# Moving the experts' weights in pieces of 4 MB instead of 2 MB

## The chip, the cores and the metric

The kernel runs on one core of one Trainium2 chip. The metric is the device time of one execution in microseconds (us). The kernel before takes 1259.34 us (median of 3 runs, 1258.63 to 1259.38).

## What is computed

One inference step of a one-layer hybrid encoder for 512 prompt tokens and 64 tokens of a running stream, model width 1024, all in float32:

```
proj = x @ w_in                                  # pool group, q, k, v, output gate, gate code
mix  = concat(pooling(u), gated_linear_attention(q, k, v, g)) @ w_out
h    = LN1(alpha * x + mix)
logits = h @ w_router + b_router                 # 32 experts, the top 4 of each token, softmax of the 4
for each expert e with its tokens:
    gate, up = split(h[tokens] @ w_gu[e] + b_gu[e])      # w_gu[e]: 1024 x 2048
    hmid = min(gate, 7) * sigmoid(1.702 * min(gate, 7)) * (clip(up, -7, 7) + 1)
    out  = hmid @ w_down[e] + b_down[e]                  # w_down[e]: 1024 x 1024
y    = LN2(alpha * h + sum over the 4 experts of weight * out)
```

Each expert has 8 MB of w_gu and 4 MB of w_down. All 32 experts are read, 384 MB.

## The kernel before, in words

The first part (projection, pooling, attention, w_out, LN1, router) takes the first 220 us. Then the experts follow in order, 0 to 31, with no branch between them; an expert has one block of at most 96 tokens (`BLK`), and further blocks, if any expert had more tokens, would be worked off in a loop behind them. Last, the rows of each token are fetched back from DRAM (`place`), summed and normalised in five groups.

**The ring.** The weights pass through SBUF in a ring of 8 slots (`RING`) of 2 MB, 16 KB per partition (`SLOT` = 4096 float32). An expert is 6 pieces (`PER`): pieces 0 to 3 are w_gu, 4 and 5 are w_down. Piece i of expert n lies in slot (6n + i) mod 8 (`piece_slot`). Each slot has a semaphore, `slot_in[s]`, that its transfer raises by 16; `landed(n, i)` is the count at which piece i of expert n is there. `EARLIER` counts the transfers of the first part (w_in) that used the same semaphores.

**Who issues.** SP issues all weight transfers, in order (`load`). Six go early, behind the last use of the ring's memory by the first part: pieces 0 to 3 of expert 0, and 0 and 1 of expert 1. Pieces 4 and 5 of expert 0 follow when the first rows of tokens are gathered. From then on each transfer waits for what lay in its slot 8 pieces before: a piece that is split is free when its two splits are done (`split_done`), piece 5, which the product reads as it is, when the down product of its expert is done (`down_read`).

**Who uses.** The multiplications run in float16 with a high and a low part. ACT makes the high part of 8 KB per partition at a time (a pair `p`, two to a piece, `hi`, L875), DVE the low part (`lo`, L1892), into 4 buffers each (`BUFS`). Of an expert pairs 0 to 7 are w_gu, 8 and 9 the first half of w_down. PE uses them in 16 units of 24 matmuls for gate and up (`unit`; units 2p and 2p+1 use pair p), and then the down product (`down`): 24 matmuls on pairs 8 and 9, and 16 float32 matmuls that read piece 5 from the ring. Before `down` of expert n PE transposes the gathered rows of expert n+1 (`rows`, L1347). DVE's order within an expert is written out in a loop at L1913: splits, with the small steps of gate and up (L1862, L1872, L1877) between them, and the low part of the next expert's rows (L1883).

**Beside it.** POOL gathers the rows of expert n+2 from DRAM (L678) and scatters the results of expert n (L691), with indirect transfers on a queue of their own (q0); the weights are on SP's (q1). Instructions are fetched over a third (q8). All share 16 DMA engines. When the down product of expert 30 is done, SP queues the loads of LN2's vectors and of `place`, behind the last weights.

Of the kernel before, what the change touches and what calls it, by code (L numbers as in the profile page):

```python
# [30 lines left out]
P = 128  # L31
D = 1024
KT = D // P
# [19 lines left out]
E = 32  # L53
# [4 lines left out]
SLOT = 4096  # L58
RING = 8
PER = 6  # L60
# [7 lines left out]
PAIRS = 10  # L68
# [6 lines left out]
def build(nc, x_prompt, x_sample, x_t, state_pool, state_gla, w_in, w_glr, w_pool, pool_scale, w_gate_up,  # L75
# [3 lines left out]
    with ExitStack() as ctx:  # L79
# [4 lines left out]
        ring = ctx.enter_context(nc.sbuf_tensor("ring", [P, RING * SLOT], F32))  # L84
# [194 lines left out]
        slot_in = [sem(f"slot_in{s}") for s in range(RING)]  # L279


        split_done, down_read = sem("split_done"), sem("down_read")
# [148 lines left out]
        def piece_slot(n, i):  # L431
            return (n * PER + i) % RING
# [6 lines left out]
        def landed(n, i):  # L439

            return 16 * (EARLIER[piece_slot(n, i)] + (n * PER + i) // RING + 1)

        def landed_again(b, i):

            return b * 16 + 16 * (EARLIER[i] + 1 + PER * E // RING)

# [24 lines left out]
        def _(sp):  # L471
# [43 lines left out]
            def load(e, i, s):  # L515

                src = w_gu[bass.ds(e, 1), i] if i < 4 else w_down[bass.ds(e, 1), i - 4]
                sp.dma_start(ring[:, s * SLOT:(s + 1) * SLOT], src.rearrange("a p n -> (a p) n"))\
                  .then_inc(slot_in[s], 16)
# [7 lines left out]
            sp.wait_ge(wo_lo, 8)  # L527
            for e, i in ((0, 0), (0, 1), (0, 2), (0, 3), (1, 0), (1, 1)):
                load(e, i, piece_slot(e, i))
# [5 lines left out]
            sp.wait_ge(gathered[0], 16)  # L535
            for i in (4, 5):
                load(0, i, piece_slot(0, i))
            for e in range(1, E):
                for i in range(2 if e == 1 else 0, PER):

                    if e == 2 and i == 0:
                        sp.dma_start(bd, b_down[0]).then_inc(bd_in, 16)

                    if i == 1:
                        sp.wait_ge(down_read, e - 1)
                    else:
                        sp.wait_ge(split_done, PAIRS * (e - 1) if i == 0 else PAIRS * (e - 1) + 2 * (i - 1))
                    load(e, i, piece_slot(e, i))
            sp.wait_ge(cnt_done, 1)
            more = sp.value_load(n_over_i[0:1, 0:1], min_val=0, max_val=E)  # L550
            with sp.If(more > 0):
                with sp.Fori(0, more) as b:
                    hold(sp, down_read, down_done(b + (E - 1)))
                    hold(sp, ov_known, b + 1)
                    e = sp.value_load(cur_i[0:1, 0:1], min_val=0, max_val=E - 1)
                    for i in range(PER):
                        load(e, i, i)
                hold(sp, down_read, down_done(more + (E - 1)))
                hold(sp, scattered, more * 16 + 16 * (E - 2))
# [173 lines left out]
        def _(act):  # L733
# [136 lines left out]
            def hi(n, p, s, got):  # L870

                if p % 2 == 0:
                    act.wait_ge(slot_in[s], got)
                act.wait_ge(unit_used, pair_done(n, p) - BUFS)
                act.activation(whi[buf(n, p)], packed(s, p), ACT.Copy, scale=W_UP).then_inc(hi_done, 1)  # L875
# [139 lines left out]
        def _(pe):  # L1015
# [359 lines left out]
            def down(n, s, got):  # L1375
# [17 lines left out]
                for k in range(first, KT):  # L1393
                    if k % 4 == 0:
                        pe.wait_ge(hm_done, n * 2 + (k // 4 + 3))
                        pe.wait_ge(slot_in[s[k // 4]], got[k // 4])
                    w = slot(s[k // 4], 4, 1024)
                    for c in range(2):
                        last = mm(out[:, c * 512:(c + 1) * 512], hm[:, k, :],
                                  w[:, k % 4, c * 512:(c + 1) * 512], k == 0, k == KT - 1)  # L1400
# [680 lines left out]
```

## Time and profile before

| | before |
|---|---|
| median of 3 runs | 1259.34 us |
| the profiled execution, its own time | 1259.37 us |
| its span on the profile | 1257.0 us |
| PE busy (weight loads) | 1192.7 us (867.1 us) |
| DVE busy | 1049.4 us |
| ACT busy | 944.6 us |
| moved by DMA | 475.17 MB, mean 378 GB/s |
| transfers of weights | 192 of 2048 KB |

Times in the rows below are from the start of the span. Busy shares are averages over parts of the kernel with different limits; what counts for this change is the stretch of the experts, from about 224 us to about 1210 us. PE's matmuls are pipelined and their ends modelled, so a busy PE isn't one at its peak. An idle time names what ended it. L1017 is the helper of all matmuls.

### The profile page before, as it was taken

To read this page: it belongs to the slowest core of one execution; us is meant where nothing else is said; L and a number is where in the kernel's file an instruction comes from. 1 tells how busy PE (TensorE), PEld (TensorE's weight loads), DVE (VectorE), ACT (ScalarE), POOL (GpSimd) and SP (SyncE) were. 2 spreads that over 40 slices of the span, in tenths; PEclk is the share of its full clock that TensorE was granted. 3 is DMA by queue.
4 is the path that set the end of the run, shared out by engine and by line. 5 is a ranking of instruction groups with operands and counts; after the bars stand their busy time and mean duration, and the time that the engine had idled before them with its cause. 6 is when DMAs were issued, how large, how long until landed. Compare 5 with 4: busy or idle time off the path is not lost.

```text
span 1257.0 us, 35029 instructions
## 1 busy us (share of the span) xinstructions
PE 1192.7 (95%) x15369; PEld 867.1 (69%) x15369; DVE 1049.4 (83%) x1209; ACT 944.6 (75%) x1260; POOL 172.2 (14%) x145
## 2 busy tenths in 40 slices
PE   7999998899999999999999999999999999999995
PEld 3555455777777777777777777777777777677752
DVE  6564577998899889898898898888888888888888
ACT  6532313688889888888888898888888888788841
POOL 1273111111000100000000011111111111111002
PEclk9999997899999999999999999999999999999998
DMA  9752491899999999999999999999999999999994
GB/s 367 291 197 86 144 406 36 355 406 421 426 425 424 424 427 424 424 425 426 425 425 425 424 426 424 424 425 426 424 426 424 425 424 425 422 422 426 409 395 139
DMA packets 47670, 475.17 MB, mean 378 GB/s; under 512 B 8781, under 2 KB 9812, under 8 KB 21660
## 3 DMA queue, kind: packets, MB, share of 16 engines
q1 hardware_dynamic: 35432, 438.69, 83.1%
q0 software_dynamic: 11392, 31.77, 6.7%
q8 instruction: 123, 2.02, 0.6%
q10 hardware_dynamic: 692, 2.43, 0.5%
q14 instruction: 31, 0.25, 0.1%
HBM read 453.17 MB, written 29.95 MB: 384 GB/s over the span
## 4 chain that ended last, share of the span: by engine, by line
PE 49%; DMA 28%; DVE 12%; issue 5%; ACT 5%; POOL 0%; DVEq 0%; SPq 0%; POOLq 0%; ACTq 0%
PE wide L1017 34%; DMA ring<-in_w_gu 16%; PE pair L1017 14%; DMA ring<-in_w_down 11%; DVE work L1892 6%; ACT work L875 3%; PE pair L1347 1%; ACT work L905 1%; DVE ring L1994 1%; DVE ring L2019 1%; DVE ring L2017 1%; DVE work L1877 0%; DMA ring<-in_x_t 0%; DVE ring L2006 0%; DMA work<-h_rows,work 0%
## 5 line engine op out<-in xcount | busy, mean ns | idle before, releaser
L1892 DVE SCALAR_TENSOR_TENSOR work<-ring,work 128x2048 f16<-128x2048 f32 x320 | 721.4, 2287 | 109.4 <-ACT work L875 94.5
L875 ACT ACTIVATE work<-ring 128x2048 f16<-128x2048 f32 x320 | 599.6, 1902 | 90.5 <-DMA ring<-in_w_gu 55.6
L1017 PE MATMUL wide<-work 128*128 128x96 f16 (+2 forms) x6970 | 465.2, 227 | 28.5 <-issue 12.6
L1017 PEld LDWEIGHTS wide<-work 128*128 128x128 f16 (+2 forms) x6970 | 364.7, 101 | 112.6 <-issue 42.2
L1017 PE MATMUL wide<-ring,work 128*96 128x512 f32 (+4 forms) x1024 | 335.1, 492 | 1.4 <-DMA ring<-part_rows 1.4
L1017 PEld LDWEIGHTS pair<-work 128*128 128x128 f16 (+2 forms) x6483 | 297.0, 100 | 34.6 <-issue 23.7
L1017 PE MATMUL pair<-work 128*128 128x96 f16 (+3 forms) x6483 | 303.5, 208 | 8.2 <-DVEq L1727 1.9
L1017 PEld LDWEIGHTS wide<-ring,work 128*96 128x96 f32 (+4 forms) x1024 | 132.0, 135 | 178.3 <-issue 125.6
L678 POOL DMA_INDIRECT work<-h_rows,work x32 | 58.4, 1826 | 477.7 <-PE pair L1347 450.4
L691 POOL DMA_INDIRECT part_rows<-work x30 | 43.1, 1438 | 373.2 <-ACT work L935 373.2
L905 ACT ACTIVATE work<-pair,work 128x96 f32<-128x96 f32 x256 | 64.8, 333 | 0.0
L905 ACT ACTIVATE work<-wide,work 128x96 f32<-128x96 f32 x256 | 64.8, 332 | 0.0
L935 ACT ACTIVATE work<-wide,work 96x1024 f32<-96x1024 f32 x30 | 33.1, 1103 | 38.6 <-PE wide L1017 38.4
L914 ACT ACTIVATE work<-work 128x384 f32<-128x384 f32 x64 | 39.4, 616 | 2.1
L921 ACT ACTIVATE work<-work 128x384 f32<-128x384 f32 x64 | 39.4, 616 | 2.1
L1872 DVE SCALAR_TENSOR_TENSOR work<-work 128x384 f32<-128x384 f32 x64 | 35.6, 556 | 1.3 <-DVE work L1862 0.2
L1347 PE MATMUL pair<-work 128*128 128x128 f32 x256 | 35.2, 282 | 0.6 <-DMA work<-h_rows,work 0.6
L1862 DVE SCALAR_TENSOR_TENSOR work<-work 128x384 f32<-128x384 f32 x64 | 35.3, 552 | 0.0
L1883 DVE SCALAR_TENSOR_TENSOR work<-pair,work 128x384 f16<-128x384 f32 x64 | 32.6, 549 | 1.1 <-ACT work L899 1.1
L1489 DVE SCALAR_TENSOR_TENSOR ring<-ring 128x1024 f16<-128x1024 f32 x16 | 19.3, 1224 | 14.2 <-ACT ring L771 13.9
L867 ACT ACTIVATE work<-pair 128x512 f32<-128x512 f32 (+1 forms) x10 | 5.0, 553 | 34.2 <-PE pair L1250 34.0
L899 ACT ACTIVATE work<-pair 128x384 f16<-128x384 f32 x64 | 27.3, 476 | 3.9 <-PE pair L1347 3.9
(211 smaller groups left out, 599.1 us busy)
## 6 DMA issues: line engine op xcount, KB each, us to landing
ring<-in_w_gu SPq DMA_DIRECT2D x128, 2048.0 KB, 29.9
ring<-in_w_down SPq DMA_DIRECT2D x64, 2048.0 KB, 30.7
part_rows<-work POOLq DMA_DIRECT2D x1, 10240.0 KB, 37.2
ring<-part_rows SPq DMA_DIRECT2D x5, 2048.0 KB, 31.4
ring<-in_w_in SPq DMA_DIRECT2D x3, 2048.0 KB
ring<-in_w_out SPq DMA_DIRECT2D x2, 2048.0 KB, 10.8
h_rows<-work POOLq DMA_DIRECT2D x1, 2560.0 KB, 9.9
ring<-h_rows SPq DMA_DIRECT2D x5, 512.0 KB, 20.0
```

The lines of the kernel that those rows point to most:

```text
L678: pool.indirect_dma_start(xg, None, h_dram, bass.IndirectOffsetOnAxis(ap=tok_i[q], axis=0), bounds_check=PLACES - 1, oob_is_err=False)\
L691: pool.indirect_dma_start(part_dram, bass.IndirectOffsetOnAxis(ap=dst_i[p], axis=0), orow, None, bounds_check=TOPK * PLACES - 1, oob_is_er ...
L875: act.activation(whi[buf(n, p)], packed(s, p), ACT.Copy, scale=W_UP).then_inc(hi_done, 1)
L905: last = act.activation(dst[:, c, :], b[:, c * BLK:(c + 1) * BLK], ACT.Relu, scale=-DOWN * S_UP, bias=bguT[:, at[0], at[1] + c:at[1] + c + 1])
L914: act.activation(sg, g1, ACT.Sigmoid, scale=-SWISH / S_UP, bias=sig_bias).then_inc(sig_done, 1)
L921: act.activation(u1, u1, ACT.Relu, scale=-1.0, bias=up_bias).then_inc(up_clip, 1)
L935: act.activation(orow, wide[1 if isinstance(n, int) else 0][0:BLK, :], ACT.Copy, scale=slots[p][:, 5:6])\
L1017: return pe.matmul(out, w, x, start=start, stop=stop, skip_group_check=True)
L1347: last = pe.transpose(bank[b][:, k * BLK:k * BLK + P], xg[:, (4 * b + k) * P:(4 * b + k + 1) * P], used)
L1862: dve.scalar_tensor_tensor(g1, g1, -LIMIT * S_UP, sg, ALU.add, ALU.mult).then_inc(gated, 1)
L1872: dve.scalar_tensor_tensor(hm[:, 4 * half:4 * half + 4, :], u1, (1.0 - LIMIT) * S_UP, g1, ALU.add, ALU.mult)\
L1892: dve.scalar_tensor_tensor(wlo[buf(n, p)], packed(s, p), W_UP, whi[buf(n, p)], ALU.mult, ALU.subtract).then_inc(split_done, 1)
```

## The change

The same bytes move in pieces of 4 MB, 32 KB per partition, each into a pair of neighbouring slots: (0,1), (2,3), (4,5), (6,7). An expert is three transfers instead of six: w_gu in two, w_down in one. In DRAM the two halves of a new piece are laid side by side for each partition (the layout is made on the host). `load` is called for even i only and writes two slots; the semaphore is that of the pair's first slot, and it is raised when all of the 4 MB are there. ACT's wait, before the high part of pairs 0, 2, 4, ..., is on that semaphore, and PE's wait for piece 5 on that of pieces 4 and 5. SP's waits are those of the later of the two slots: for the pair that held pieces 4 and 5 of an expert the end of its down product, else the second split of its second piece. The splits, their buffers and all matmuls stay as they are.

```diff
--- before.py
+++ after.py
@@ -438,11 +438,11 @@
 
         def landed(n, i):
 
-            return 16 * (EARLIER[piece_slot(n, i)] + (n * PER + i) // RING + 1)
+            return 16 * (EARLIER[piece_slot(n, i) // 2 * 2] + (n * PER + i) // RING + 1)
 
         def landed_again(b, i):
 
-            return b * 16 + 16 * (EARLIER[i] + 1 + PER * E // RING)
+            return b * 16 + 16 * (EARLIER[i // 2 * 2] + 1 + PER * E // RING)
 
         def pairs(n):
 
@@ -514,8 +514,8 @@
 
             def load(e, i, s):
 
-                src = w_gu[bass.ds(e, 1), i] if i < 4 else w_down[bass.ds(e, 1), i - 4]
-                sp.dma_start(ring[:, s * SLOT:(s + 1) * SLOT], src.rearrange("a p n -> (a p) n"))\
+                src = w_gu[bass.ds(e, 1), i // 2] if i < 4 else w_down[bass.ds(e, 1)]
+                sp.dma_start(ring[:, s * SLOT:(s + 2) * SLOT], src.rearrange("a p n -> (a p) n"))\
                   .then_inc(slot_in[s], 16)
 
             sp.wait_ge(o_norm, TILES)
@@ -525,7 +525,7 @@
             sp.wait_ge(z_out, 8)
             sp.wait_ge(states_out, 96)
             sp.wait_ge(wo_lo, 8)
-            for e, i in ((0, 0), (0, 1), (0, 2), (0, 3), (1, 0), (1, 1)):
+            for e, i in ((0, 0), (0, 2), (1, 0)):
                 load(e, i, piece_slot(e, i))
             sp.wait_ge(hT_ready, 2 * TILES)
             sp.wait_ge(h_stored, 16 * TILES)
@@ -533,18 +533,17 @@
 
             sp.wait_ge(mix_ready, TILES)
             sp.wait_ge(gathered[0], 16)
-            for i in (4, 5):
-                load(0, i, piece_slot(0, i))
+            load(0, 4, piece_slot(0, 4))
             for e in range(1, E):
-                for i in range(2 if e == 1 else 0, PER):
+                for i in range(2 if e == 1 else 0, PER, 2):
 
                     if e == 2 and i == 0:
                         sp.dma_start(bd, b_down[0]).then_inc(bd_in, 16)
 
-                    if i == 1:
+                    if i == 0:
                         sp.wait_ge(down_read, e - 1)
                     else:
-                        sp.wait_ge(split_done, PAIRS * (e - 1) if i == 0 else PAIRS * (e - 1) + 2 * (i - 1))
+                        sp.wait_ge(split_done, PAIRS * (e - 1) + 2 * i)
                     load(e, i, piece_slot(e, i))
             sp.wait_ge(cnt_done, 1)
             more = sp.value_load(n_over_i[0:1, 0:1], min_val=0, max_val=E)
@@ -553,7 +552,7 @@
                     hold(sp, down_read, down_done(b + (E - 1)))
                     hold(sp, ov_known, b + 1)
                     e = sp.value_load(cur_i[0:1, 0:1], min_val=0, max_val=E - 1)
-                    for i in range(PER):
+                    for i in range(0, PER, 2):
                         load(e, i, i)
                 hold(sp, down_read, down_done(more + (E - 1)))
                 hold(sp, scattered, more * 16 + 16 * (E - 2))
@@ -870,7 +869,7 @@
             def hi(n, p, s, got):
 
                 if p % 2 == 0:
-                    act.wait_ge(slot_in[s], got)
+                    act.wait_ge(slot_in[s // 2 * 2], got)
                 act.wait_ge(unit_used, pair_done(n, p) - BUFS)
                 act.activation(whi[buf(n, p)], packed(s, p), ACT.Copy, scale=W_UP).then_inc(hi_done, 1)
 
@@ -1393,7 +1392,7 @@
                 for k in range(first, KT):
                     if k % 4 == 0:
                         pe.wait_ge(hm_done, n * 2 + (k // 4 + 3))
-                        pe.wait_ge(slot_in[s[k // 4]], got[k // 4])
+                        pe.wait_ge(slot_in[s[0]], got[0])
                     w = slot(s[k // 4], 4, 1024)
                     for c in range(2):
                         last = mm(out[:, c * 512:(c + 1) * 512], hm[:, k, :],
@@ -2060,10 +2059,10 @@
     laid["w_out"] = np.asarray(inputs["w_out"])[0].reshape(2, 4, P, D).transpose(0, 2, 1, 3)
 
     laid["w_gu"] = np.asarray(inputs["w_gu"]).reshape(E, KT, P, 2, 2, 4, P).transpose(0, 4, 3, 2, 5, 1, 6)\
-        .reshape(E, 4, P, SLOT)
-
-    laid["w_down"] = np.asarray(inputs["w_down"]).reshape(E, 2, 4, P, D).transpose(0, 1, 3, 2, 4)\
-        .reshape(E, 2, P, SLOT)
+        .reshape(E, 2, 2, P, SLOT).transpose(0, 1, 3, 2, 4).reshape(E, 2, P, 2 * SLOT)
+
+    laid["w_down"] = np.asarray(inputs["w_down"]).reshape(E, KT, P, D).transpose(0, 2, 1, 3)\
+        .reshape(E, P, 2 * SLOT)
 
     laid["b_gu"] = np.asarray(inputs["b_gu"]).reshape(E, 16, P).transpose(2, 0, 1)
```

## Rows read from the trace of the kernel before

**Rows 1.** The page: slices of the span, and the queue of the weights (packets, MB, share).

```profile
DMA  9752491899999999999999999999999999999994
GB/s 367 291 197 86 144 406 36 355 406 421 426 425 424 424 427 424 424 425 426 425 425 425 424 426 424 424 425 426 424 426 424 425 424 425 422 422 426 409 395 139
q1 hardware_dynamic: 35432, 438.69, 83.1%
```

**Rows 2.** A window: length, PE, PEld, DVE, ACT, POOL busy, PEclk, DMA share, GB/s.

```profile
900.00:1000.00 100.00, 96.21 (x1400) 73.56 (x1399) 86.96 (x92) 84.97 (x105) 11.86 (x6) 1.00 1.01 425
```

**Rows 3.** The chain that ended last, experts 5 and 6: start, us, what.

```profile
402.25 12.25 PE wide L1017 x40
...
432.77 12.25 PE wide L1017 x40
```

**Rows 4.** ACT's timeline, experts 27 and 31: start, us, what, idle before and releaser.

```profile
1052.73 1.91 ACT L875 ACTIVATE work<-ring 128x2048 f16<-128x2048 f32 x1 [2.31 <-DMA ring<-in_w_gu]
...
1178.89 1.91 ACT L875 ACTIVATE work<-ring 128x2048 f16<-128x2048 f32 x1 [2.52 <-DMA ring<-in_w_gu]
...
1183.79 3.71 ACT L875 ACTIVATE work<-ring 128x2048 f16<-128x2048 f32 x2 [0.42 <-DMA ring<-in_w_gu]
```

**Rows 5.** Timelines of SP and ACT, the first loads.

```profile
0.81 0.43 SPq L474 DMA_DIRECT2D ring<-in_w_in  x1
...
4.93 1.06 ACT L771 ACTIVATE ring<-ring 128x1024 f16<-128x1024 f32 x1 [2.84 <-DMA ring<-in_w_in]
...
8.03 1.16 ACT L776 ACTIVATE work<-ring 128x1152 f16<-128x1152 f32 x1 [0.28 <-DMA ring<-in_x_t]
9.46 1.16 ACT L776 ACTIVATE work<-ring 128x1152 f16<-128x1152 f32 x1 [0.27 <-DMA ring<-in_x_t]
```

**Rows 6.** Expert 0: an issue and its landing, PE's and SP's timeline, the chain.

```profile
L518 SPq DMA_DIRECT2D ring<-in_w_down x1: 328/328/328, 240.2 to 240.2; - x1
...
DMA to landing us min/median/max: 13.3/13.3/13.3
...
247.17 1.07 PE L1347 MATMUL pair<-work 128*128 128x128 f32 x8
...
248.78 12.25 PE wide L1017 x40
...
250.90 10.96 SPq L518 DMA_DIRECT2D ring<-in_w_gu  x3
```

**Rows 7.** Gathers: the first (alone), the second, and those of 300 to 1180 us.

```profile
DMA to landing us min/median/max: 4.7/4.7/4.7
...
227.04 1.04 POOL L678 DMA_INDIRECT work<-h_rows,work  x1 [5.34 <-PE pair L1347]
...
DMA to landing us min/median/max: 10.5/11.9/12.9
```

**Rows 8.** The chain, expert 27: w_down taken up, and the down product.

```profile
1075.48 1.92 ACT work L875
...
1080.28 13.93 PE wide L1017 x40
```

**Rows 9.** The timeline of the last expert: DVE's steps, and PE's down product.

```profile
1183.05 1.01 DVE L1883 SCALAR_TENSOR_TENSOR work<-pair,work 128x384 f16<-128x384 f32 x2
...
1184.48 8.88 DVE L1892 SCALAR_TENSOR_TENSOR work<-ring,work 128x2048 f16<-128x2048 f32 x4
...
1193.29 1.27 DVE L1919 SCALAR_TENSOR_TENSOR work<-wide,work 96x1024 f16<-96x1024 f32 x1
...
1204.23 0.55 DVE L1877 SCALAR_TENSOR_TENSOR work<-work 128x384 f16<-128x384 f32 x1
...
1204.88 5.38 PE L1017 MATMUL wide<-work 128*96 128x512 f16 x24 [0.97 <-DVE work L1877]
```

**Rows 10.** DMA queues of 225 to 1180 us: packets, MB, share of 16 engines.

```profile
q0 software_dynamic: 7824, 18.04, 4.9%
q8 instruction: 107, 1.75, 0.7%
```

## The prediction, made before the changed kernel was run

> **What bounds the kernel now.** I read the page's slices first: from the tenth to the 37th the DMA digit is 9 and the rate stays at 421 to 427 GB/s [rows 1]. A window of 100 us sharpens it: the 16 DMA engines are busy the whole time, at 425 GB/s, beside a PE at 96, a DVE at 87 and an ACT at 85 [rows 2]. So from 224 us, when the second batch of weights starts, until the last weights land, the time is set by bytes. The compute is only slightly faster. In a stretch where the data are early, one expert takes 30.52 us (402.25 to 432.77 in the chain) [rows 3]. In a stretch where ACT waits for each piece, the first piece of an expert is taken up at 1052.73 (expert 27) and at 1178.89 (expert 31): 126.16 / 4 = 31.54 us per expert [rows 4]. The reader is to see two things: anything that leaves the DMA engines idle between 224 us and the last landing is paid in full, and the compute has 1.0 us of spare time in each expert, so a late start on the last expert isn't made up.
>
> **The rate (the term that gains).** The change sends the same bytes in half the transfers and half the rows. A 2 MB piece gives each of 16 engines 8 rows of 16 KB; with no gather on the queue two landings are 4.90 us apart (ACT starts at 1178.89 and 1183.79) [rows 4]. The x_t loads give each engine 8 rows of 4,608 bytes: landings 1.43 us apart (8.03, 9.46) [rows 5]. Two sizes with equal rows give the fixed part: bytes per engine 131,072 and 36,864; slope (4.90 - 1.43) / 94,208 = 0.0368 us per 1,000 bytes; fixed 1.43 - 36.9 x 0.0368 = 0.07 us (0.08 if either spacing is 0.01 off). Doubling the row saves that once per pair of old pieces. Of 96 new transfers 93 lie behind 224 us: 93 x 0.07 = 6.5 us. Bounds: 0, if a 32 KB row is cut in two again, and 7.5 us at 0.08. No row here is longer than 16 KB, so this is the largest unknown; I take 6.5, because each piece shows as exactly 128 large packets, one per row (35,432 packets for 438.69 MB) [rows 1].
> The Trainium skill (DMA: Bandwidth & Descriptors, Anatomy of one DMA) gives about 2 us fixed plus bytes at 436 GB/s for a transfer. The spacing above, 4.9 us where that rule has 6.8, shows that queued transfers here overlap all but 0.07 of it; by the rule the saving would be 96 x 2 = 192 us.
>
> **Issue times, start of the ring.** In the new order the wait for a pair of slots is that of its later half. (1,2) goes at the fourth split instead of the second, (1,4) at the eighth instead of the sixth: 5 us later each, behind work that still fills the queue. The exception is the pair whose old content is the down weights. Before, (2,0) is issued at 250.90, after the tenth split; (2,1) is the second of the three issues that follow, at the end of the down product, 248.78 + 12.25 = 261.03 [rows 6]. Now both go at 261.03. What is ahead: (1,4), issued 240.2, lands 13.3 us later [rows 6], at 253.5, and (1,5) 4.9 to 5.8 us on, 258.4 to 259.3; a gather shares the queue, so I say 259.5. A transfer into an empty queue has a start-up: the first w_in block is issued at 0.81 and taken up at 4.93 [rows 5], 4.1 us, of which its 512 KB take 1.2: 2.9. So the stream resumes at 261.03 + 2.9 = 263.9: idle for about 4 us (2.5 to 5.5 by the uncertainty of both ends). It is paid, as the DMA bounds the rest. The same pair of the next expert is released some 31 us later, at 292, and could be moving at 295; the stream, already 4 us late, is busy until 259.5 + 4 + 31.5 = 295: no second gap worth a term, and each further expert widens the cover by 31.5 - 30.5 = 1.0 us.
>
> **Gathers.** Alone a gather lands in 4.7 us; among weights in 11.9 (10.5 to 12.9) [rows 7]: about 7 us of waiting behind 16 KB rows. With rows of 32 KB I expect 7 more, 19. Each is issued right behind the transposes of one expert and wanted at those of the next, about 30 us on: hidden. Only the second, issued 227.0, has less: wanted at 247.17 [rows 6, 7], while 227 + 19 = 246. Cost nothing; were the cover gone, it would lengthen the gap above one for one, which the 5.5 holds. The Trainium skill (same page, Queues, rings and completion order) says that an engine changes between queues only at packet borders; the two gather times agree, and by it the doubling would be as reckoned.
>
> **The tail (the term that loses).** Both halves of a pair now raise one semaphore, so the first half is known one piece, 4.9 us, later. While the stream flows nothing is lost, as slots are refilled in time: at expert 27 w_down's first half is taken up at 1075.48, the down product ends at 1080.28 + 13.93 = 1094.21 [rows 8], 18.7 us later and about 13.8 behind the second half. Now that is some 19 behind the pair's landing, with three transfers (31.5 us) queued behind it: margin 31.5 - 19 - 2.9 = 9.6 us. At the end it is lost. For expert 31, DVE can begin when pieces 0 and 1 are there, 1183.79, and ACT has done 1.91: 1185.70. Up to the last f16 operand of the down product it has 9 splits at the pace of four in 8.88 (20.0), two f16 halves of the rows (1.0), places (the 0.4 between 1184.06 and 1184.48), the 1.27 of the previous expert's result, and three steps of 0.55 that overlap their neighbours a little (1.5): 24.2 us in a row [rows 9]. End 1209.9 against 1204.8 now, where the last of these steps (1204.23, 0.55) lets PE start at 1204.88 [rows 9]: 5.1, and with short waits between I take +5.5. PE is no help: its down product of expert 30 shifts by about as much. Bounds: 4.9 (one piece, if DVE has the rest to spare) and 7.5 (if the backlog of expert 30 adds to it). What follows the down product (PE's last sums, DVE's adding and normalising) starts from it; its loads are queued right behind the weights and land no later than now by more than the stream does, so the shift passes through.
> SP issues half as many transfers and queues nothing else in that time but b_down: nothing. ACT and PE run the same instructions, with some waits on another semaphore: nothing, hidden under DMA or DVE. The host's layout isn't in the time.
>
> **Sum.** The profiled execution took 1259.37 (span 1257.0 and 2.4 around it), against a median of 1259.34: no correction. 1259.4 + 4.0 - 6.5 + 5.5 = 1262.4. Ends of all terms: 1259.4 + 2.5 - 7.5 + 4.9 = 1259.3, and 1259.4 + 5.5 - 0 + 7.5 = 1272.4.
>
> **Rivals.**
> A. Long rows save nothing (cut to 16 KB): 1259.4 + 4.0 + 5.5 = 1268.9. For it: no longer row is seen; against: one packet per row so far. 0.18.
> B, other side: the fixed cost is larger than the quiet spacing tells. An expert takes 31.54, six quiet pieces 29.4, so 2.1 us go elsewhere; the gathers' and scatters' 18.04 MB over the 30.3 experts of that window are 0.60 MB or 1.4 us, instruction fetches (1.75 MB) 0.15 us [rows 10]. The 0.55 us left may be interruptions that go with the number of rows or transfers. If half vanishes: 31 x 0.28 = 9 us, 1253.4. It decides from 0.18 us per expert (1262.4 - 31 x 0.18 = 1256.8). For it: I can't place the 0.55; against: it may as well grow with long rows. 0.20.
> C. Four pairs starve the stream: the margin of 9.6 us is used up in some experts (the split chain, held until a whole pair is there, lags). At 0.5 us per expert 15 us more: 1278. Against: the margin. 0.11.
> D. The fixed cost is paid once per transfer, 2.9 us as in the start-up row: 1259.4 - 96 x 2.9 = 981. The rule of the Trainium skill cited above reads so; the quiet spacing contradicts it. 0.01.
>
> **From this to the numbers.** My own case has 0.50, 1259 to 1266. A change under 0.2% (2.5 us: 1256.8 to 1261.9) is about what can't be told from none. Of the 0.50 some 0.20 falls into that band. Faster: 0.20 + 0.01 = 0.21. Same: 0.20. Slower: 0.30 + 0.18 + 0.11 = 0.59. The range leaves out C and the lower half of B: 1253 to 1271; my case with A alone would be 1259 to 1271.
>
> **What would show it.** Rate: packets of 32 KB, quiet landings of pairs 9.7 us apart instead of 9.8. Start: a dip of the DMA share between 259 and 264. Ring: DMA share 1.0 from 270 to 1170. Gathers: landing near 19 us. Tail: the last w_down within 3 us of 1203.4 (now 1183.79 + 4 x 4.9), the last down product starting about 7 us behind it (now 1.5). I am wrong if a second gap shows (C), if packets stay at 16 KB (A), or if an expert takes under 31.1 us (B).

## The result, and the profile after

The changed kernel takes 1263.86 us (median of 5 runs, 1263.16 to 1265.51) against 1258.63 (5 runs, 1256.65 to 1259.38): a ratio of 1.0043, 95% interval 1.003 to 1.0056. Run again beside later experiments it was 1263.00 against 1258.95, 1.0030 (1.0019 to 1.0041). So it is 4 to 5 us slower, more than the 0.2% that counts as a difference here. The forecast was 1262.4, in a range of 1253 to 1271, with "slower" as the likeliest sign.

The profiled execution of the changed kernel took 1265.51, with a span of 1263.7. That is the longest of the five, so its trace holds a little more than the median does; what the second trace doesn't repeat is marked below.

From the page of the changed kernel: the slices, the weights' queue, the chain's shares by engine, and the issues of the weights. Behind SP's loads line numbers are one lower than before (L1016 is what was L1017).

```profile
DMA  9752491989999999999999999999999999999993
GB/s 357 301 193 86 166 383 34 359 365 417 389 417 430 424 419 428 432 429 427 424 429 426 417 427 429 428 428 426 429 426 427 426 423 427 425 428 428 419 390 105
...
q1 hardware_dynamic: 21608, 438.68, 82.3%
...
PE 84%; DVE 6%; DMA 5%; issue 3%; ACT 1%; POOL 0%; SPq 0%; DVEq 0%; POOLq 0%
...
ring<-in_w_gu SPq DMA_DIRECT2D x64, 4096.0 KB, 23.4
ring<-in_w_down SPq DMA_DIRECT2D x32, 4096.0 KB, 25.6
```

Three readings beside [rows 1]. The packets fell by 13,824. Of these 12,288 are the rows: 96 transfers of 128 instead of 192. The other 1,536 are 96 x 16, the small packets (under 512 B) that close a transfer on each of 16 engines. So a row of 32 KB is one packet. The rate of most slices of the flat part rose from between 424 and 426 GB/s to between 426 and 429, though single slices now fall to 417. Slices 9 and 11 fell to 365 and 389, where before they had 406 and 426. These slices, 253 to 284 us and 316 to 348 us, hold the start of the ring. And the chain changed its owner: before it was PE 49%, DMA 28%, DVE 12%, now PE 84%, DMA 5%.

**The start.** SP's timeline of the changed kernel, then windows of the same stretch (length, PE, PEld, DVE, ACT, POOL busy, PEclk, DMA share, GB/s).

```profile
245.12 0.33 SPq L518 DMA_DIRECT2D ring<-in_w_down  x1
...
261.46 2.07 SPq L518 DMA_DIRECT2D ring<-in_w_gu  x2
```

```profile
258.00:260.00 2.00, 2.00 (x6) 0.67 (x5) 2.00 (x2) 1.01 (x1) 0.00 (x0) 1.00 0.34 103
260.00:262.00 2.00, 2.00 (x22) 1.14 (x21) 2.00 (x2) 0.53 (x1) 0.00 (x0) 1.00 0.05 16
262.00:264.00 2.00, 2.00 (x52) 2.00 (x50) 1.98 (x6) 1.01 (x2) 0.51 (x1) 1.00 0.94 262
...
324.00:326.00 2.00, 2.00 (x6) 0.74 (x5) 2.00 (x2) 0.00 (x0) 0.00 (x0) 1.00 0.77 326
326.00:328.00 2.00, 2.00 (x29) 1.33 (x28) 2.00 (x3) 0.87 (x1) 0.00 (x0) 1.00 0.08 31
```

The issue that came at 250.90 [rows 6] comes at 261.46, and the queue is empty by then: the shares leave 2 x (0.66 + 0.95 + 0.06) = 3.3 us of idle DMA between 258 and 264 (before, the three shares were 1.02, 0.97 and 1.05). A second hole follows two experts later, 2 x (0.23 + 0.92) = 2.3 us at 326.

**The tail.** ACT's timeline, then DVE's, then the chain of the last expert of the changed kernel.

```profile
1185.73 1.91 ACT L874 ACTIVATE work<-ring 128x2048 f16<-128x2048 f32 x1 [2.56 <-DMA ring<-in_w_gu]
...
1195.44 1.91 ACT L874 ACTIVATE work<-ring 128x2048 f16<-128x2048 f32 x1 [0.65 <-DMA ring<-in_w_gu]
```

```profile
1191.32 8.88 DVE L1891 SCALAR_TENSOR_TENSOR work<-ring,work 128x2048 f16<-128x2048 f32 x4
...
1211.06 0.55 DVE L1876 SCALAR_TENSOR_TENSOR work<-work 128x384 f16<-128x384 f32 x1
```

```profile
1209.56 1.50 issue
1211.06 0.56 DVE work L1876
1211.62 0.09 issue
1211.71 12.25 PE wide L1016 x40
```

The pair is taken up at 1185.73; before, its second half was there at 1183.79 [rows 4], so the stream itself is 1.94 us late. The step of 0.55 us that frees the down product stood at 1204.23 and is now at 1211.06 [rows 9]; the product starts at 1211.71 instead of 1204.88, 6.83 later. Of these, 1.94 come from the stream and 4.89 from the tail. The last weights tell the same: they landed at 1203.4 before and at 1205.2 now (the last increment of their semaphore), and the product starts 6.5 behind that instead of 1.5. The spans differ by 1263.7 - 1257.0 = 6.7, so nothing is lost or won behind it. Take-up to down product: 26.0 us now (1185.73 to 1211.71), 21.1 before.

### The profile page after: what moved, and what is told of

Its sections match the earlier page's. It is cut to its first block, busy times and chain, and to the rows that moved or that the text cites. A ratio compares the mean times of both kernels' runs of the same rounds, so it can differ in the third digit from the quotient of the medians.

```text
span 1263.7 us, 34933 instructions
## 1 busy us (share of the span) xinstructions
PE 1191.1 (94%) x15369; PEld 869.3 (69%) x15369; DVE 1049.6 (83%) x1209; ACT 944.8 (75%) x1260; POOL 155.3 (12%) x145
## 4 chain that ended last, share of the span: by engine, by line
PE 84%; DVE 6%; DMA 5%; issue 3%; ACT 1%; POOL 0%; SPq 0%; DVEq 0%; POOLq 0%
PE wide L1016 58%; PE pair L1016 23%; DMA ring<-in_w_gu 4%; PE pair L1346 2%; DVE work L1891 1%; DVE ring L1993 1%; DVE ring L2018 1%; DVE ring L2016 1%; DMA ring<-in_x_t 0%; DVE ring L2005 0%; DMA work<-h_rows,work 0%; ACT work L874 0%; POOL work L664 0%; DVE work L1756 0%; DVE work L1766 0%
## 5 line engine op out<-in xcount | busy, mean ns | idle before, releaser
L874 ACT ACTIVATE work<-ring 128x2048 f16<-128x2048 f32 x320 | 598.2, 1902 | 71.4 <-DMA ring<-in_w_gu 37.4
L1016 PE MATMUL wide<-work 128*128 128x96 f16 (+2 forms) x6970 | 464.3, 227 | 31.9 <-issue 28.9
L1016 PEld LDWEIGHTS wide<-work 128*128 128x128 f16 (+2 forms) x6970 | 366.2, 101 | 112.4 <-issue 42.5
L1016 PE MATMUL wide<-ring,work 128*96 128x512 f32 (+4 forms) x1024 | 334.9, 492 | 0.0
L1016 PEld LDWEIGHTS pair<-work 128*128 128x128 f16 (+2 forms) x6483 | 297.5, 101 | 36.7 <-issue 26.2
L1016 PE MATMUL pair<-work 128*128 128x96 f16 (+3 forms) x6483 | 304.6, 208 | 9.7 <-issue 1.9
L1016 PEld LDWEIGHTS wide<-ring,work 128*96 128x96 f32 (+4 forms) x1024 | 132.2, 135 | 176.3 <-issue 125.6
L677 POOL DMA_INDIRECT work<-h_rows,work x32 | 43.5, 1361 | 515.2 <-PE pair L1346 485.6
L1346 PEld LDWEIGHTS pair<-work 128*128 128x128 f32 x256 | 28.2, 144 | 4.5 <-issue 4.5
L1488 DVE SCALAR_TENSOR_TENSOR ring<-ring 128x1024 f16<-128x1024 f32 x16 | 19.3, 1222 | 14.3 <-ACT ring L770 14.0
```

The source lines that it names most:

```text
L677: pool.indirect_dma_start(xg, None, h_dram, bass.IndirectOffsetOnAxis(ap=tok_i[q], axis=0), bounds_check=PLACES - 1, oob_is_err=False)\
L1016: return pe.matmul(out, w, x, start=start, stop=stop, skip_group_check=True)
L1346: last = pe.transpose(bank[b][:, k * BLK:k * BLK + P], xg[:, (4 * b + k) * P:(4 * b + k + 1) * P], used)
```

## The experiments

### The two new delays, each alone

In e2_order the kernel before keeps its 2 MB transfers and its semaphores; only SP's waits are those of the change.

```diff
-                for i in range(2 if e == 1 else 0, PER):
+                for i in range(2 if e == 1 else 0, PER, 2):
...
-                    if i == 1:
+                    if i == 0:
                         sp.wait_ge(down_read, e - 1)
                     else:
-                        sp.wait_ge(split_done, PAIRS * (e - 1) if i == 0 else PAIRS * (e - 1) + 2 * (i - 1))
+                        sp.wait_ge(split_done, PAIRS * (e - 1) + 2 * i)
                     load(e, i, piece_slot(e, i))
+                    load(e, i + 1, piece_slot(e, i + 1))
```

> The kernel before, 2 MB transfers and its own semaphores, with only the issue times changed: both transfers of a pair are issued when the later slot is free, as in the changed kernel. My account: the DMA engines idle 3 to 4 us near 260 us, nothing else changes, no gain of rate, no later tail: 1258.6 + 4 = 1262.6. If the later second gap (near 326 us) comes from the order and not from the rows: 1264 to 1265. If the start costs nothing: 1258.6.

Measured: 1263.85 against 1258.94, 1.0039 (1.0025 to 1.0053), +4.9 us. Its windows:

```profile
258.00:260.00 2.00, 2.00 (x6) 0.77 (x5) 2.00 (x2) 1.91 (x2) 0.00 (x0) 1.00 0.72 256
260.00:262.00 2.00, 2.00 (x10) 0.77 (x9) 2.00 (x2) 0.00 (x0) 0.00 (x0) 1.00 0.13 47
262.00:264.00 2.00, 2.00 (x52) 2.00 (x50) 2.00 (x2) 1.11 (x1) 0.00 (x0) 1.00 0.64 139
```

The hole is there with rows of 16 KB too: 2 x (0.28 + 0.87 + 0.36) = 3.0 us of idle DMA. The 139 GB/s of the third window, at a share of 0.64, shows that the queue also needs a while to come up to its rate. From 250 to 360 us all queues moved 44.47 MB against 46.05 before, which is 3.7 us at 425 GB/s. The last weights landed 5.1 us later (1208.5 against 1203.4), and the last down product followed 1.5 us behind them, as before. So the whole loss is the stream's, and about 1 us of it comes later and isn't placed.

In e3_wait the transfers and their order are those of before; only ACT waits for the second half of each pair before it takes up the first, as the one semaphore of the change makes it.

```diff
             def next_hi(n, p):
+                if p % 4 == 0:
+                    act.wait_ge(slot_in[piece_slot(n, p // 2 + 1)], landed(n, p // 2 + 1))
                 hi(n, p, piece_slot(n, p // 2), landed(n, p // 2))
```

> The kernel before with one more wait: ACT takes up the first piece of a pair only when both have landed. My account: nothing is lost while the stream flows, and the last down product starts 5 us later: 1258.6 + 5 = 1263.6. If the cover of the ring is less than reckoned (four pairs starve the stream), more than 1268. If DVE makes the start up, 1259.

Measured: 1263.04 against 1258.94, 1.0035 (1.0023 to 1.0048), +4.1 us by the medians. The chain at the last down product:

```profile
1208.50 0.56 DVE work L1879
1209.06 0.09 issue
1209.15 13.16 PE wide L1019 x44
```

1209.15 against 1204.88 [rows 9]: 4.3 us later. The last weights landed no later than before (1202.7 against 1203.4), so the wait costs only at the tail, as forecast.

### What the number of transfers and the length of the rows are worth

e1_rows16 is the changed kernel, order, semaphores and 96 transfers of 4 MB alike, but each transfer has 256 rows of 16 KB.

```diff
-                src = w_gu[bass.ds(e, 1), i // 2] if i < 4 else w_down[bass.ds(e, 1)]
-                sp.dma_start(ring[:, s * SLOT:(s + 2) * SLOT], src.rearrange("a p n -> (a p) n"))\
+                src = w_gu[bass.ds(e, 1), i:i + 2] if i < 4 else w_down[bass.ds(e, 1)]
+                sp.dma_start(ring[:, s * SLOT:(s + 2) * SLOT].rearrange("p (t n) -> p t n", t=2),
+                             src.rearrange("a t p n -> (a p) t n"))\
```

> The changed kernel with its 4 MB transfers, issue times and waits, but DRAM laid out as before, so that each transfer moves rows of 16 KB (two per partition). If the rate's gain goes with the length of the rows, nearly all of the 6 us are lost again: about 1269 us, with weights at 425 GB/s. If it goes with the number of transfers, it stays at 1264. A second theory, from the trace of the changed kernel: long rows also hold up PE's instruction fetches (PE waits 'issue' before the wide matmuls 28.9 us there, 12.6 before) and lengthen the compute of an expert from 30.4 to 30.9 us. By it these waits go back to about 13 us here, gathers land in 12 us instead of 18 or so, and the dip of the DMA share near 326 us is gone, so that only 4 us of start remain: about 1266.

Measured: 1268.49 against 1258.94, 1.0075 (1.0056 to 1.0093). That is +9.5 us. e2_order and e3_wait together make 1.0039 x 1.0035 = 1.0074. So the two delays add up, and 96 transfers in place of 192, with equal rows, save nothing that can be measured. The intervals of the three ratios together leave room for about 3 us either way. The length of the rows alone is e1_rows16 against the changed kernel: 1268.49 - 1263.86 = 4.6 us, or 5.5 against the second set of runs. By ratios it is 1.0075 - 1.0043 = 0.0032, 4.0 us, or 5.7. So it lies between 4 and 6 by the medians, with an uncertainty of some 2 us. The traces say the same of the stream: with equal waits the last weights landed at 1208.4 with rows of 16 KB and at 1205.2 and 1203.5 (two traces) with rows of 32 KB.

The other direction is e7_rows8: the kernel before, its 192 transfers and its order, with rows of 8 KB (two per partition and piece; the host lays the halves apart).

```diff
-                sp.dma_start(ring[:, s * SLOT:(s + 1) * SLOT], src.rearrange("a p n -> (a p) n"))\
+                sp.dma_start(ring[:, s * SLOT:(s + 1) * SLOT].rearrange("p (t n) -> p t n", t=2),
+                             src.rearrange("a t p n -> (a p) t n"))\
```

> The kernel before with rows of 8 KB in the same 192 transfers: the other side of the row term. If the fixed 0.07 us per transfer is 8 rows of 9 ns: 186 transfers x 0.07 = 13 us more, 1271.6. If it is one cost per transfer: 1258.6. If long rows hold up instruction fetches, PE's issue waits fall below the 12.6 us of before; if not, they stay.

Measured: 1271.36 against 1258.94, 1.0096 (1.0079 to 1.0112), +12.4 us. The fixed part of 0.07 us for each 8 rows of an engine, taken from [rows 4, 5], gives 186 x 0.07 = 13.0. The DMA totals of 500 to 1100 us, for 8 KB, 16 KB (before) and 32 KB (changed):

```profile
DMA packets 35987, 251.52 MB, mean 419 GB/s; under 512 B 3976, under 2 KB 3976, under 8 KB 6728
```

```profile
DMA packets 21695, 254.89 MB, mean 425 GB/s; under 512 B 4042, under 2 KB 4042, under 8 KB 6828
```

```profile
DMA packets 13375, 255.75 MB, mean 426 GB/s; under 512 B 3080, under 2 KB 3080, under 8 KB 5875
```

From 8 to 16 KB the rate rises by 1.3%. From 16 to 32 KB it should rise by half of that, 0.67%, if the cost goes by the row. In this trace it rises by 0.34%, in the second trace of the changed kernel (after_again, below: 254.98 MB) by nothing; against e1_rows16, which has the same waits (253.99 MB), by 0.7 and 0.4%. So one window is too coarse to tell. The packets are sharper: the median time of a packet of the weights is 312, 612 and 1213 ns for 8, 16 and 32 KB, so each doubling saves the same 11 to 12 ns per long packet. (Records of packets overlap a little, so this shows that the saving goes on, not its price in the stream's time.) And the DMA share from 500 to 1100 us is 1.00 in the changed kernel: its engines don't idle there. Whatever takes back part of the gain isn't a new limit of the stream.

### Mending the delays, with long rows kept

If the only fault of the change were the two delays, it could have the gain without the loss. In e4_both the 4 MB transfers stay, except that the first pair of experts 2 to 6 and all pairs of experts 30 and 31 move as two transfers of 2 MB, each with its own semaphore, issued when its own slot is free.

```diff
+        def halves(e, i):
+            return i == 0 and 2 <= e < 7 or e >= E - 2
...
+                    if halves(e, i):
+                        sp.wait_ge(split_done, PAIRS * (e - 1) if i == 0 else PAIRS * (e - 1) + 2 * (i - 1))
+                        load_half(e, i, piece_slot(e, i))
                     if i == 0:
                         sp.wait_ge(down_read, e - 1)
                     else:
                         sp.wait_ge(split_done, PAIRS * (e - 1) + 2 * i)
-                    load(e, i, piece_slot(e, i))
+                    if halves(e, i):
+                        load_half(e, i + 1, piece_slot(e, i + 1))
+                    else:
+                        load(e, i, piece_slot(e, i))
```

> The changed kernel, but with the first pair of experts 2 to 6 and all pairs of experts 30 and 31 moved as two transfers of 2 MB with their own semaphores, at the issue times of the kernel before. My account (order 4.9, wait 4.1, long rows' rate -6.6, and a second gap of 2 us near 326 us from PE's late instructions, which the fuller queue should cover): the gaps and the late tail go, 11 of 93 long transfers are lost (0.8 us): 1258.9 - 6.6 + 0.8 = 1253. If PE's late instructions cost more than the second gap: 1256 to 1259.

Measured: 1259.42 against 1258.95 (11 and 30 runs), 1.0004 (0.9993 to 1.0016). The delays are gone, at the tail for instance (chain of e4_both):

```profile
1203.99 13.14 PE wide L1040 x44
```

1203.99 against 1204.88 [rows 9]. Yet only 3.6 us were won against the changed kernel run beside it (1263.00), where two mended delays of 4 to 5 us each should give 9. The parts one by one:

In e5_start only the start is mended, in e6_tail only the tail.

```diff
-            return i == 0 and 2 <= e < 7 or e >= E - 2
+            return i == 0 and 2 <= e < 7
```

> The changed kernel with only the first pair of experts 2 to 6 in two transfers. My account: the idle stretches near 260, 294 and 326 us go (4.9 + 2 us), 5 long transfers are lost (0.4): 1263.9 - 6.9 + 0.4 = 1257.4. If the second gap stays, as it is not a matter of the queue: 1259.4.

```diff
-            return i == 0 and 2 <= e < 7 or e >= E - 2
+            return e >= E - 2
```

> The changed kernel with only experts 30 and 31 in 2 MB transfers with their own semaphores. My account: the last down product starts 4 us earlier, six long transfers are lost (0.4): 1263.9 - 4.1 + 0.4 = 1260.2. If the wait for whole pairs cost its 4.1 us all along the stream and not at the end: 1264.

> The changed kernel once more, for a second trace. If the idle stretch near 326 us and PE's issue waits of 29 us belong to it, they return (over 24 us of issue waits, a dip of 1.5 us or more); if they were an accident of one execution, 16 us or less and no dip. Time 1263.9.

Measured, against 1258.95: e5_start 1261.08, 1.0017 (1.0005 to 1.003); e6_tail 1261.19, 1.0020 (1.0008 to 1.0032); the changed kernel again (after_again) 1263.00, 1.0030. By the medians each half of the mending gives 1.8 to 1.9 us of its 4 to 5, with an uncertainty of about 2 us; that the two together give less than 9 is clear of it.

after_again also gave a second trace. Its windows at 326 us have no hole:

```profile
326.00:328.00 2.00, 2.00 (x51) 2.00 (x49) 0.35 (x1) 1.93 (x2) 0.53 (x1) 1.00 1.09 412
```

So the second hole belongs to the one execution in which expert 2 was slow (PE stopped for 0.71 and 2.00 us there). It is not part of the change's usual price.

The hole at 258 is in both traces. Where the halves end, with expert 7, a hole opens in turn. One window each of e4_both and e5_start:

```profile
414.00:416.00 2.00, 2.00 (x33) 1.40 (x32) 2.00 (x2) 1.07 (x1) 0.00 (x0) 1.00 0.71 246
```

```profile
414.00:416.00 2.00, 2.00 (x6) 0.81 (x5) 2.00 (x2) 0.00 (x0) 0.00 (x0) 1.00 0.32 133
```

The late issue for the pair behind the down weights was only put off. In e9_half_13 the halves last until expert 12; e10_long_late goes further and, but for the three issued first and w_down of expert 0, uses whole 4 MB pairs only for experts 12 to 29. Both edits are against e4_both.

```diff
-            return i == 0 and 2 <= e < 7 or e >= E - 2
+            return i == 0 and 2 <= e < 13 or e >= E - 2
```

> As the run with both mended (4 MB transfers, halves for the first pair of experts 2 to 6 and all of 30 and 31), but the first pair moves in halves up to expert 12. My account: the idle stretch only moved to expert 7 there (1.6 us near 414 us, 3.1 in the sister run), since the cover behind the late issue was still short; from expert 13 it is some 9 us and no stretch stays idle: 1 to 2 us less, 1257.5 to 1258.5. PE's issue waits stay near 25 us and hold the compute near 31 us per expert, so no more than that is gained. If the stream were still the bound: 1253.

```diff
-            return i == 0 and 2 <= e < 7 or e >= E - 2
+            return 2 <= e < 12 or e == 1 and i > 0 or e >= E - 2
```

> Long rows only where the compute has time to spare: 2 MB transfers for experts 1 to 11, 30 and 31, 4 MB transfers for 12 to 29. My account: PE's issue waits fall to about 18 us (12.6 with none, 30 with all), no idle stretch, the stream gains 18 x 0.25 = 4 us, no longer tail: 1255. If the late instructions take it all back even so: 1258 to 1259.

Measured, against 1259.03 (29 runs): e9_half_13 1257.58, 0.9988 (0.9977 to 0.9999); e10_long_late 1257.60, 0.9990 (0.9981 to 0.9999). The window of e9_half_13 at the place of the holes above:

```profile
414.00:416.00 2.00, 2.00 (x6) 0.61 (x5) 2.00 (x2) 0.00 (x0) 0.00 (x0) 1.00 0.94 395
```

The hole is gone, and the median is another 1.8 us lower. That the one comes from the other isn't shown: the intervals overlap, and in the traces the last weights land no earlier than in e4_both (1199.2 against 1198.9). The two beat the kernel before by 0.1%, by the edge of their intervals: under the 0.2% that I call a difference. Against the kernel before 1.4 us are left of the 4 to 6 that long rows save.

### A shorter tail for the kernel before

If a larger last piece costs at the tail, a smaller one might pay. e8_fine_tail is the kernel before, with the last expert's six pieces moved as two halves of 1 MB each, with a semaphore for each half.

```diff
+                if isinstance(e, int) and e == E - 1:
+                    for j, done in enumerate((slot_in[s], fine_in[i])):
+                        sp.dma_start(ring[:, s * SLOT + j * SLOT // 2:s * SLOT + (j + 1) * SLOT // 2],
+                                     src[:, j * SLOT // 2:(j + 1) * SLOT // 2]).then_inc(done, 16)
```

> The kernel before, with the six pieces of the last expert moved in halves of 1 MB (rows of 8 KB), each half with its own semaphore: the tail term with the opposite sign. My account: the first half is known 2.4 us earlier, DVE starts the last expert earlier: 2 us less, 0.4 us for the short rows: 1257.3. If the end of the last expert depends on the last landing and not on the first: 1259 to 1259.5.

Measured: 1257.89 against 1259.03, 0.9994 (0.9985 to 1.0002). A miss: no difference can be told. Its chain at the end:

```profile
1191.94 29.39 DMA ring<-part_rows
```

In its profiled execution the last expert is not on the chain at all; the fetch of the partial rows for the final sums ended later. But that execution took 1259.22, 1.3 above the median, and its last down product began at 1205.33, no earlier than the 1204.88 of before. So the trace doesn't show a shorter tail, and why a finer last piece gives so little stays open.

## Where the missing gain went

Long rows save DMA time, but the chain of the changed kernel is PE's. The groups of waits of the changed kernel (us in total, times, longest), then the same for 8 KB rows:

```profile
ACT work L874 <- DMA ring<-in_w_gu: 37.4, 20, 3.6
...
PE wide L1016 <- issue: 28.9, 32, 2.0
```

```profile
ACT work L876 <- DMA ring<-in_w_gu: 89.4, 61, 4.2
...
PE wide L1018 <- issue: 7.8, 12, 1.7
```

And of the kernel before, which the prediction hadn't read:

```profile
ACT work L875 <- DMA ring<-in_w_gu: 55.6, 43, 3.9
...
PE wide L1017 <- issue: 12.6, 20, 1.4
```

ACT waits less and less for weights: 89.4, 55.6, 37.4 us with rows of 8, 16, 32 KB (24.6 in after_again; with the changed kernel's own waits and 16 KB rows, e1_rows16, it is 87.2). That is the gain. But PE's idle time that no semaphore ends ("issue") grows: 7.8, 12.6, 28.9 (30.4 in after_again). It isn't the order or the wait: with 16 KB rows e1_rows16 has 10.6, e2_order 15.6, e3_wait 8.9. With long rows in nearly all transfers e5_start has 28.8 and e6_tail 26.8; with shorter rows in a part of them e4_both has 18.9, e9_half_13 20.7, e10_long_late 20.9. Each is one trace, and equal rows differ by up to 7 us, so only the steps between row lengths count. In the changed kernel these stops lie in the middle of a unit's matmuls, where PE waits for no data. The chain shows one, and then the period of an expert:

```profile
302.06 4.91 PE wide L1016 x113
306.97 2.00 issue
...
315.02 12.08 PE wide L1016 x40
...
345.82 12.08 PE wide L1016 x40
...
376.63 12.07 PE wide L1016 x40
...
778.76 12.08 PE wide L1016 x40
```

From 376.63 to 778.76 are 13 experts: 402.13 / 13 = 30.93 us each, where the kernel before had 30.52 [rows 3]; by the ends of 15 down products it is (790.84 - 357.90) / 14 = 30.92, against (717.93 - 292.41) / 14 = 30.39 before. The extra stops, (28.9 - 12.6) / 31 = 0.53 us per expert, are the whole of that difference; in these very stretches PE's stops of this kind are 14.3 and 6.0 us, 0.59 per expert apart. The stream takes 31.3 us per expert now (w_down of experts 5 and 29 landed at 391.7 and 1141.9 in after_again), so the compute's reserve against it, 1.0 us per expert before, is about 31.3 - 30.9 = 0.4.

**What holds PE back.** Instructions come over a queue of their own (q8) through the same 16 DMA engines [rows 10], in packets of 16 KB, one for every 127 matmuls with their weight loads (13,545 matmuls and 106 packets from 225 to 1180 us). The packed trace holds the time of each packet. The queue's row for 306.5 to 306.6 us, and PE's timeline of the stop shown above:

```profile
q8 instruction: 1, 0.02, 58.5%
```

```profile
308.96 0.81 PE L1016 MATMUL wide<-work 128*128 128x96 f16 x10 [2.00 <-issue]
```

That packet began at 306.57 and ended at 307.50; PE ran dry at 306.97 and went on at 308.96, 1.46 behind the packet's end. It is the same for all 37 of PE's stops of this kind between 225 and 1215 us: each ended 1.24 to 1.62 us after the end of a q8 packet, and the stops lie whole multiples of 127 matmuls apart, as many as packets came between (to within one matmul). Before it holds for 19 of 19 (1.26 to 1.61), with 8 KB rows for 11 of 11, and over all 13 traces 362 of 373 stops end 1.1 to 1.75 us behind a packet, where packets are some 9 us apart. So the stops are late instructions. How late they come goes with the rows: from PE's first matmul of a block to the start of the packet with the next block it takes 3.1 us in the median with rows of 8 KB, 3.3 to 3.5 with 16 KB (four kernels) and 3.7 to 3.8 with 32 KB (three), and from the packet's end until PE needs it 2.7, 1.9 to 2.1 and 1.6 to 1.7 are left.

The other small transfers also suffer from long rows. The gathers among the weights (from 300 to 1180 us) in after_again, issue to landing:

```profile
DMA to landing us min/median/max: 15.1/15.9/16.9
```

11.9 before [rows 7], 12.5 in e1_rows16, which has 4 MB transfers too, but rows of 16 KB. The scatters went from 10.9 to 14.4. So a small transfer waits longer behind longer rows: 4 us more for one of POOL's. That the instruction packets wait at the same place is argued from the shared engines and the order of the three row lengths.

**What that does to the mending.** From each trace, the time at which the last weights landed (last increment of their semaphore), the start of the last down product, and the difference:

| | landed | product | behind |
|---|---|---|---|
| before | 1203.4 | 1204.9 | 1.5 |
| e2_order | 1208.5 | 1210.0 | 1.5 |
| e3_wait | 1202.7 | 1209.2 | 6.4 |
| e1_rows16 | 1208.4 | 1214.8 | 6.4 |
| changed, two traces | 1205.2, 1203.5 | 1211.7, 1210.0 | 6.5, 6.5 |
| e5_start | 1200.8 | 1208.2 | 7.4 |
| e6_tail | 1204.2 | 1208.3 | 4.1 |
| e4_both | 1198.9 | 1204.0 | 5.1 |
| e9_half_13 | 1199.2 | 1203.4 | 4.2 |
| e10_long_late | 1202.1 | 1206.1 | 4.0 |

In e4_both and e9_half_13 the long rows do bring the last weights 4.2 to 4.5 us earlier than before. But the last product follows 4 to 5 us behind them, not 1.5. Two things keep it there. The one is the reserve above. In e5_start there is no DMA on the chain between 260 and 1195 us at all: with the start mended, its chain is PE's for 88% of the span. The other is how late the tail was mended. Up to expert 29 whole pairs keep the compute 5 to 6 us behind the stream (the down product of expert 29 starts 5.5 behind its weights in e6_tail, 5.2 in e10_long_late); when the halves begin with expert 30, two experts are left to make up 4.9 us. They make up 1.4 to 2.5. A reserve of 1.0 us per expert would not do it in two experts either. No run began the halves of the tail earlier, so what each of the two costs isn't shown.

## Why the prediction was right, and where its sum was off

The sign and the size were right, and of the three terms two are close:

- **Start, 4.0.** The late issue is at 261.46 (said: 261.03), the idle DMA is 3.3 us (said: about 4, between 259 and 264), and the order alone costs 4.9 us. The bounds were 2.5 to 5.5. No second gap: right in the second trace; in the first there was one, behind an unusually slow expert, because the cover was thinner than I had reckoned.
- **Tail, 5.5.** The wait alone costs 4.1 by the medians, 4.3 at the down product; in the changed kernel it is 4.89. That is the lower bound, one old piece; the 0.6 for short waits and backlog wasn't needed. The last w_down was issued at 1177.2 and landed 28.0 us later, at 1205.2 (said: 1203.4, within 3), and the down product began 6.5 behind it (said: 7).
- **Rate, -6.5.** This is the step that was mis-sized. The fixed part of a row was right: 8 KB rows cost 12.4 us against 13.0, and a packet of 32 KB saves as many ns against two of 16 KB as one of 16 KB against two of 8 KB. One packet per row was right. Two quiet pair landings are 1195.44 - 1185.73 = 9.71 us apart (said: 9.7 instead of 9.8). But "93 x 0.07 = 6.5" took the DMA engines as the only limit; measured, the longer rows are worth 4 to 6 us with the delays of the change in place, and in e9_half_13, with 76 of 93 transfers long and the delays mended as far as they were, 1.4 are left. The prediction had read "1.0 us of spare time in each expert" as a fixed quantity, and put ACT and PE, "the same instructions", at nothing. Long rows made PE's instructions late and took 0.5 to 0.6 us per expert of that spare time.
- **Gathers, 19 us.** 15.9: four more, not seven; hidden all the same. The prediction looked at the gathers as the only small transfers that share the DMA engines. The Trainium skill (DMA: Bandwidth & Descriptors, Queues, rings and completion order) says that an engine changes between queues only at packet borders. By that rule any short transfer, on any queue, should suffer from longer packets; the gathers, the scatters and the instruction packets here agree with it in direction, and the rise of the gathers is under the doubling that I had taken from it.
- **The sum.** With the measured terms: 4.9 + 4.1 less 4 to 6 is 3 to 5 us; measured were 3.8 and 5.4 by the two ratios. This isn't a check of its own, as the 4 to 6 was itself taken from the changed kernel's time. I had 3.0. The start was 0.9 too small, the tail up to 1.4 and the gain of the rate up to 2.5 too large, and these partly cancel: the total is closer than its terms, and that much of it is luck.

The rivals: A (long rows save nothing, 1268.9) is out: packets are of 32 KB, and e1_rows16, in which A is made true, came to 1268.49, 0.4 us from its price. B (a hidden cost per row, 1253.4) is out: 8 KB rows would have cost more than the fixed part allows, and they cost 0.6 less; and the stream's 31.3 us per expert are above B's mark of 31.1. C (four pairs starve the stream, 1278) is out: from the tenth slice on the DMA digits stay at 9, and the first hole is the only one in both traces. But its neighbour was true: not the stream but the compute lost 0.5 us per expert, and most of that was hidden by the reserve. D (a fixed cost once per transfer, 981) is out: half the transfers at equal rows changed nothing. The Trainium skill (same page, Anatomy of one DMA) gives about 2 us fixed for a transfer, fitted on transfers issued from GpSimd; e1_rows16 shows that in SP's queue, which behind the first hole isn't empty, nothing near it is paid (96 x 2 would be 192 us).

What stays open: how much of the mended tail's missing part is PE's late instructions and how much that the halves began only two experts before the end; why e8_fine_tail gained nothing clear; and where the last 1 us of e2_order lies. A kernel with long rows and a way to keep the instruction fetches off the weights' engines wasn't tried, nor one with halves for the last eight or ten experts, nor transfers with long rows on only some partitions.

## What to carry to other kernels

Making the transfers of a ring larger has three prices apart from the rate: the data are known later by one old piece (paid once, at the end: 4 us), a slot pair is free later (paid wherever the queue runs dry, here once: 5 us), and other small transfers wait longer behind longer rows. The gain of doubling 2 MB transfers is in the rows, not in the number of transfers; here it was 1% of the time from 8 to 16 KB and 0.3 to 0.5% from 16 to 32 KB. And when the bound is only 3% ahead of the next one, reckon the next one anew under the change: a spare of 1 us in 31 is not a constant. Such a spare is also all that makes up a delay: by an estimate from these numbers 4.9 us take five experts at 1 us each, so a cure of the tail has to begin at least that early. That wasn't tried.

## What was unexpected of the hardware

- PE's stops without a semaphore are late instructions: in the changed kernel's first trace all 37, over all traces 362 of 373, end 1.1 to 1.75 us behind a 16 KB packet of the instruction queue. They grow with the row length of a stream that PE has nothing to do with, 7.8, 12.6 and 28.9 to 30.4 us at 8, 16 and 32 KB, enough to lengthen each expert by about 0.5 us.
- Doubling the row from 16 to 32 KB lengthens a gather by 4 us (11.9 to 15.9), while doubling the transfer at equal rows lengthens it by 0.6 (12.5).
- 192 against 96 transfers at equal rows: 1.0075, where order and wait alone make 1.0074, to within about 3 us.
